# Expert one-hots of a PEER layer in 16-bit token pairs on VectorE, with a ScalarE copy of the left one, on one Trainium2 core

## The chip, the core and the metric

The kernel runs on one core of a Trainium2 chip. The metric is the device time of one execution, in microseconds (us). Of the core's engines four compute here: TensorE (PE in the profile; PEld is its weight load), VectorE (DVE), ScalarE (ACT) and GpSimd (POOL). The queue of SyncE (SP) streams weights, and some transfers are issued from the ACT and POOL queues.

## What is computed

A first block (feed-forward, token mixer, feed-forward) and then two layers of attention with a product-key expert layer ("PEER") run on 256 tokens of width 1024. The change touches the expert layer, plus the table of distances that the attention adds. Cut to what matters:

```python
PEER_HEADS, PEER_NKEYS, PEER_TOPK = 8, 128, 16        # 128 * 128 experts
scores = einsum("thpd,hpnd->thpn", q, sub_keys)       # two halves p of a key
top_v, top_i = lax.top_k(scores, PEER_TOPK)
cand_v = top_v[:, :, 0, :, None] + top_v[:, :, 1, None, :]
best_v, best_pos = lax.top_k(cand_v, PEER_TOPK)       # 16 experts per head
expert_idx = take_along_axis(cand_i, best_pos)        # = i0 * 128 + i1
gates = softmax(best_v)
a = gelu(einsum("td,thkd->thk", h, expert_u[expert_idx]))
y = einsum("thk,thkd->td", gates * a, expert_v[expert_idx])
```

## The kernel before

The kernel gathers no expert. It computes all 128 x 128 of them densely: weights arrive as units of 128x1024 f32, each is split into a high part (`w_hi`, by ScalarE, L390, called from `hi`) and the rest (`w_lo`, by VectorE, L728, called from `lo`), and TensorE multiplies high and low parts with the high and low parts of the activations (`product`, L1443, L1444 and L1447, for U; `v_unit`, L1837 and L1843, for V). There are two buffers of each, so `step(u)` on ScalarE and VectorE is the split of unit u+2: ScalarE's waits until TensorE has used unit u (`used`), VectorE's for ScalarE's (`w_hi_ready`), and TensorE's low pass for VectorE's (`w_taken`). The expert activations of a layer fill the arena, `experts[partition i0][n = i1][token]`.

What makes the dense sum the reference's is a matrix of gates: for each token a 128 x 128 matrix over (i0, i1) that holds the gate at the 128 chosen experts (8 heads x 16) and zero elsewhere. It is the product of two one-hot matrices over those 128 choices, made by TensorE for one token at a time: the left one (128 choices x 128 values of i0) is the stationary operand, the right one (128 choices x 64 values of i1, one half of the keys), weighed by the gate, is the moving operand. The gate is split in three bf16 parts, so there are three matmuls per token (L1811, 128x64). Tokens are taken in groups of 8, 32 groups to a half of the keys; a group is called a turn. Every turn goes with two weight units, and a layer has four stages:

- peer_a: U units 0 to 63, beside the top-k on VectorE.
- peer_b: U units 64 to 127, with 32 turns that make the gates of keys 0 to 63 and multiply them into `experts`. These are the u turns.
- peer_c: V units 0 to 63, with 32 turns for keys 64 to 127. These are the v turns.
- peer_d: V units 64 to 127, without turns.

In a turn of the kernel before, VectorE builds the right one-hot `hot_eq` (128x512) and the left one-hot `hot_l` (128x1024) by comparing f32 keys with f32 numbers (`build`, L1237); GpSimd multiplies `hot_eq` by the three gate parts (`weigh`, L1417); TensorE makes 24 matmuls (`token_gates`, L1811), and VectorE multiplies their result into `experts` (`multiply`, L1247). There is one buffer of `hot_l`, `hot_eq` and `hot_r`; the result has two (the banks `st` 2 and 3). The result lies token by token, 64 keys in a row each, while `experts` has the tokens in a row and the next key 256 elements on.

The orders are written by hand. VectorE in a u turn g (`u_turn`, L1264): right one-hot, `lo` of unit 2g+2, multiply of turn g-1, left one-hot, `lo` of unit 2g+3. In a v turn (`v_turn`, L1273) the low part of the activations, `lower` (L1253), stands before the right and before the left one-hot. TensorE (`turns`): unit 2g, gates of turn g-1, unit 2g+1, unit 2g+2, gates of turn g, unit 2g+3, and so on. ScalarE in a u turn: per unit a Gelu (L657) and a `hi` (L390); in a v turn: per unit a copy of the activations' high part, `upper` (L691), and a `hi`.

Of the kernel before, what the change touches and what calls it, by code (L numbers as in the profile page):

```python
# [92 lines left out]
def _layout1():  # L93
    at = 0
    for name, n in (("ident", 128), ("ones", 128), ("iota", 128), ("dist", TT * T), ("onecol", 31),
                    ("iota16", 16), ("eps", 1), ("qk_scale", 1), ("qk_eps", 1)):
        _K1[name] = (at, n)
        at += n
    return at
# [20 lines left out]
EXTRA = 3328  # L120


def build(nc, weights, ada_weights, params, const1, const2, smallw, out):
    with ExitStack() as ctx:
# [44 lines left out]
        def ar(at, *shape, base=None):  # L169
# [4 lines left out]
            elif len(shape) == 3:  # L174
# [11 lines left out]
        dist = kc("dist")  # L186
# [97 lines left out]
        selt = ar(512, 3, T, base=extra)  # L284

        gate_rest = ar(1280, 2, T, base=extra)
        gate_parts = ar(1792, 384, base=extra).bitcast(BF16).rearrange("p (k t) -> p k t", k=3)
        hot_l = ar(2176, 512, base=extra).bitcast(BF16).rearrange("p (t n) -> p t n", t=GROUP)
        hot_eq = ar(2688, 256, base=extra).bitcast(BF16).rearrange("p (t n) -> p t n", t=GROUP)
        hot_r = [ar(at, 256, base=extra).bitcast(BF16).rearrange("p (t n) -> p t n", t=GROUP)  # L290
                 for at in (2944, 1280, 1536)]
# [89 lines left out]
        def _(eng):  # L381
            link = linker(eng, "act_chain")
            nc_a = nc.scalar
            eng.dma_start(k1[:, :], const1).then_inc(sem("k1_in"), 16)
# [202 lines left out]
            for l in range(LAYERS):  # L587
# [83 lines left out]

                def gates_exp():
# [10 lines left out]
                u_half(HALF)  # L683
# [9 lines left out]
                def v_half(first):  # L693
# [3 lines left out]
                    with eng.Fori(0, HALF // 4 - 1) as i:  # L697
                        for k in range(4):
                            eng.wait_ge(used, plus(i, 4, nth(v_base + first + k)))
                            upper(first + k + 2, i)  # L700
                            step(v_base + first + k, i, 4)

                    for n in range(first + HALF - 4, first + HALF):
# [3 lines left out]
                        step(v_base + n)  # L707

                v_half(0)
# [10 lines left out]
        def _(eng):  # L720
# [335 lines left out]
            for l in range(LAYERS):  # L1056
# [9 lines left out]
                stage(eng, ST[f"proj{l}"])  # L1066
                for h in range(AH):
# [158 lines left out]
                def build(k, half, g, i=None):  # L1226
# [765 lines left out]
```

## Time and profile before

| | us |
|---|---|
| median of 3 runs | 3389.08 (3388.97 to 3389.96) |
| profiled execution, own time | 3391.32 |
| its span in the trace | 3389.6 |
| busy: PE, PEld | 3020.5 (89%), 2756.0 (81%) |
| busy: DVE, ACT, POOL | 2484.9 (73%), 1358.3 (40%), 750.7 (22%) |
| stages peer_b of the two layers (turns with U) | about 1543 to 1763 and 2726 to 2950 |
| stages peer_c (turns with V) | about 1771 to 2008 and 2958 to 3195 |
| mean granted TensorE clock | 0.935 of full speed |

The span is the time from the first to the last instruction in the trace; the execution's own time is 1.7 us longer. An engine's busy time is the union of its instructions. Idle time of an engine is given with what ended it. The stages above are found by where the one-hot instructions (L1237) begin and end.

### The profile page before, as it was taken

To read this page: it belongs to the slowest core of one execution; us is meant where nothing else is said; L and a number is where in the kernel's file an instruction comes from. 1 tells how busy PE (TensorE), PEld (TensorE's weight loads), DVE (VectorE), ACT (ScalarE), POOL (GpSimd) and SP (SyncE) were. 2 spreads that over 40 slices of the span, in tenths; PEclk is the share of its full clock that TensorE was granted. 3 is DMA by queue.
4 is the path that set the end of the run, shared out by engine and by line. 5 is a ranking of instruction groups with operands and counts; after the bars stand their busy time and mean duration, and the time that the engine had idled before them with its cause. 6 is when DMAs were issued, how large, how long until landed. Compare 5 with 4: busy or idle time off the path is not lost. (4 is left out here: it accounts for less than half of the span.)

```text
span 3389.6 us, 62057 instructions
## 1 busy us (share of the span) xinstructions
PE 3020.5 (89%) x22464; PEld 2756.0 (81%) x22464; DVE 2484.9 (73%) x3349; ACT 1358.3 (40%) x1958; POOL 750.7 (22%) x588
## 2 busy tenths in 40 slices
PE   3998988889989778999998889998799999988898
PEld 2998976779979578989987668796799899866687
DVE  6777734357778566998999986644449889899865
ACT  2434532234344334544333335543345443333354
POOL 1011002101101000025765530000000256655300
PEclk7999986889989689999999999997899999999999
DMA  7784520048858345544444445552245444444454
GB/s 270 270 278 139 185 100 1 1 147 276 278 199 316 103 153 176 174 159 144 153 137 148 137 143 192 166 171 78 100 148 174 156 149 149 136 146 139 143 192 143
DMA packets 149585, 547.98 MB, mean 162 GB/s; under 512 B 16608, under 2 KB 16736, under 8 KB 149088
## 3 DMA queue, kind: packets, MB, share of 16 engines
q1 hardware_dynamic: 124704, 454.29, 39.8%
q0 software_dynamic: 24336, 89.14, 7.8%
q10 hardware_dynamic: 432, 2.97, 0.2%
q8 instruction: 79, 1.29, 0.2%
q14 instruction: 34, 0.28, 0.0%
HBM read 545.29 MB, written 1.05 MB: 161 GB/s over the span
## 5 line engine op out<-in xcount | busy, mean ns | idle before, releaser
L728 DVE TENSOR_TENSOR w_lo<-ring,w_hi 128x1024 fp32r<-128x1024 f32 x864 | 1140.4, 1321 | 542.8 <-ACT w_hi L390 539.9
L390 ACT ACTIVATE w_hi<-ring 128x1024 fp32r<-128x1024 f32 x864 | 910.8, 1054 | 1105.7 <-PE st L1447 915.6
L1443 PE MATMUL st<-h_hi,w_hi 128*128 128x256 f32 x4064 | 1038.7, 292 | 43.1 <-DVE h_lo L757 27.0
L1444 PE MATMUL st<-h_lo,w_hi 128*128 128x256 f32 x4064 | 1016.6, 287 | 0.0
L1443 PEld LDWEIGHTS st<-h_hi,w_hi 128*128 128x128 f32 x4064 | 793.7, 195 | 62.8 <-issue 38.6
L1444 PEld LDWEIGHTS st<-h_lo,w_hi 128*128 128x128 f32 x4064 | 796.2, 196 | 1.0
L1417 POOL TENSOR_TENSOR extra<-extra 128x512 bf16<-128x512 bf16 x384 | 565.7, 1499 | 429.5 <-DVE extra L1237 429.5
L1447 PE MATMUL st<-h_hi,w_lo 128*128 128x256 f32 x4064 | 581.9, 287 | 23.1 <-DVE w_lo L728 22.8
L1447 PEld LDWEIGHTS st<-h_hi,w_lo 128*128 128x128 f32 x4064 | 532.7, 195 | 29.5 <-DVE w_lo L728 29.3
L1237 DVE TENSOR_TENSOR extra<-extra,k 128x512 bf16<-128x512 f32 (+1 forms) x256 | 334.1, 1305 | 5.3 <-PE st L1811 2.8
L1837 PE MATMUL acc<-w_hi,act_hi 128*128 128x512 f32 x1024 | 325.4, 399 | 4.9 <-DVE act_lo L1253 4.9
L1837 PE MATMUL acc<-w_hi,act_lo 128*128 128x512 f32 x1024 | 319.5, 393 | 0.0
L691 ACT ACTIVATE act_hi<-arena 128x256 fp32r (+1 forms) x256 | 106.6, 418 | 487.1 <-PE acc L1843 470.5
L1843 PE MATMUL acc<-w_lo,act_hi 128*128 128x512 f32 x1024 | 275.5, 391 | 0.0
L1332 POOL DMA_DIRECT2D arena<-ada_weights x156 | 82.4, 528 | 815.1 <-DVE arena L782 443.9
L1837 PEld LDWEIGHTS acc<-w_hi,act_lo 128*128 128x128 f32 x1024 | 194.5, 190 | 41.5
L1843 PEld LDWEIGHTS acc<-w_lo,act_hi 128*128 128x128 f32 x1024 | 193.9, 189 | 41.1
L1837 PEld LDWEIGHTS acc<-w_hi,act_hi 128*128 128x128 f32 x1024 | 189.7, 191 | 42.7 <-issue 5.1
L1253 DVE TENSOR_TENSOR act_lo<-arena,act_hi 128x256 fp32r<-128x256 f32 x256 | 127.9, 501 | 117.1 <-ACT act_hi L691 114.7
L1811 PEld LDWEIGHTS st<-extra 128*128 128x128 bf16 x3072 | 97.6, 98 | 118.4 <-issue 94.2
L1811 PE MATMUL st<-extra 128*128 128x64 bf16 x3072 | 112.4, 194 | 79.4 <-DVE extra L1237 68.8
L1247 DVE TENSOR_TENSOR arena<-arena,st 128x512 f32 (+1 forms) x128 | 170.9, 1335 | 0.8 <-PE st L1811 0.8
(254 smaller groups left out, 3060.4 us busy)
## 6 DMA issues: line engine op xcount, KB each, us to landing
ring<-weights SPq DMA_DIRECT2D x864, 512.0 KB, 3.3
arena<-ada_weights POOLq DMA_DIRECT2D x168, 512.0 KB, 5.1
arena<-const ACTq DMA_DIRECT2D x1, 2112.0 KB, 8.7
x_t<-params SPq DMA_DIRECT2D x1, 1024.0 KB, 8.3
out<-arena POOLq DMA_DIRECT2D x1, 1024.0 KB, 4.2
k<-const ACTq DMA_DIRECT2D x1, 473.0 KB, 4.6
arena<-smallw ACTq DMA_DIRECT2D x1, 320.0 KB, 10.4
par<-params SPq DMA_DIRECT2D x1, 198.5 KB, 4.4
```

Source lines behind the costliest of these rows:

```text
L390: nc_a.activation(w_hi[:, u % 2, :], ring[:, u % RING, :], ACT.Copy).then_inc(hi_ready, 1)
L728: v.tensor_tensor(w_lo[:, u % 2, :], ring[:, u % RING, :], w_hi[:, u % 2, :], ALU.subtract)\
L1237: v.tensor_tensor(dst, selt[:, k, at].unsqueeze(2).to_broadcast([P, GROUP, width]), numbers.unsqueeze(1).to_broadcast([P, GROUP, width]), ...
L1247: v.tensor_tensor(here, here, st[:, 2 + g % 2, :].rearrange("p (t n) -> p t n", t=GROUP), ALU.mult).then_inc(sem("g_mult"), 1)
L1253: v.tensor_tensor(act_lo[:, n % 2, :], src, act_hi[:, n % 2, :], ALU.subtract) .then_inc(sem("gated_lo"), 1)
L1417: g.tensor_tensor(hot_r[k], hot_eq, gate_parts[:, k, at].unsqueeze(2) .to_broadcast([P, GROUP, HALF]), ALU.mult).then_inc(sem("hot_r"), 1)
L1443: mm(dst(t), w, hi_t(t), start=start, stop=False, skip_group_check=True)
L1444: mm(dst(t), w, lo_t(t), start=False, stop=False, skip_group_check=True)
L1447: ins = mm(dst(t), w_lo[:, u % 2, t * P:(t + 1) * P], hi_t(t), start=False, stop=last and (t == DT - 1 or not shared), skip_group_check=True)
L1811: ins = mm(st[:, 2 + g % 2, k * HALF:(k + 1) * HALF], hot_l[:, k, :], hot_r[part_][:, k, :], start=part_ == 0, stop=part_ == 2)
L1837: mm(acc[:, 2 * t + half, :], act_part[:, b, t * P:(t + 1) * P], w_hi[:, u % 2, 512 * half:512 * half + 512], start=False, stop=False, ski ...
L1843: ins = mm(acc[:, 2 * t + half, :], act_hi[:, b, t * P:(t + 1) * P], w_lo[:, u % 2, 512 * half:512 * half + 512], start=False, stop=last, ...
```

## The change

Both one-hots become bf16 throughout. Keys are copied out of PSUM as bf16 (`keys_t`), the numbers 0 to 127 are kept twice side by side in bf16 (`pair_iota`), and two tokens lie innermost in each one-hot, `[4 pairs of tokens][keys][2 tokens]`. The weighing moves from GpSimd to VectorE (`weigh`, three products of 128x512), and there are two buffers of the weighed right one-hots and of the left one. The left one-hot is built in pairs too (`hot_pair`, one buffer), and ScalarE copies it into rows that are contiguous per token (`by_token`), from which TensorE loads its weights. TensorE reads the right one-hot in steps of two elements and writes the result with the 8 tokens innermost, in steps of 8 f32, so that `multiply` runs over tokens in rows of 8. The table of distances moves out of the constants that stay loaded: it is loaded at the beginning of each attention layer into the arena, from the POOL queue, and VectorE waits for it (`dist_in`). The diff, cut:

```diff
-EXTRA = 3328
+EXTRA = 3840
+DIST_AT = 26112
...
-        dist = kc("dist")
+        dist = ar(DIST_AT, TT * T)
...
+        hot_l = [ar(512 * b, 512, base=extra).bitcast(BF16).rearrange("p (t n) -> p t n", t=GROUP) for b in range(2)]
+        hot_r = [[hots(1024 + 768 * b + 256 * k, 256) for k in range(3)] for b in range(2)]
+        hot_pair = hots(3328, 512)
...
+        keys_t = ar(2944, 256, base=extra).bitcast(BF16).rearrange("p (k t) -> p k t", k=2)
+        pair_iota = ar(3200, 128, base=extra).bitcast(BF16).rearrange("p (n r) -> p n r", r=2)
...
-            eng.dma_start(k1[:, :], const1).then_inc(sem("k1_in"), 16)
+            eng.dma_start(k1[:, :], const1[:, 0:N_K1]).then_inc(sem("k1_in"), 16)
...
+                def by_token(half, g, i=None):
+
+                    n = 2 * TURNS * l + TURNS * half + g
+                    eng.wait_ge(sem("hot_pair"), plus(i, 2, n + 1))
+                    if n >= 2:
+                        eng.wait_ge(sem("g_psum"), plus(i, 2, n - 1))
+                    nc_a.activation(hot_l[g % 2].rearrange("p (q r) n -> p q n r", r=2), hot_pair, ACT.Copy)\
+                        .then_inc(sem("hot_l"), 1)
...
                             gelu_of(first + k, i)
                             step(base + first + k + 1, i, 4)
+                            if turns and k % 2 == 0:
+                                by_token(0, k // 2, i)
...
-                nc_a.activation(selt, st[:, 2:4, :].rearrange("p a b -> p (a b)")[:, 0:3 * T]
-                                .rearrange("p (k t) -> p k t", k=3), ACT.Copy).then_inc(sem("selt"), 1)
+                nc_a.activation(keys_t, st[:, 2, :].rearrange("p (k t) -> p k t", k=2), ACT.Copy)
+                nc_a.activation(gate_t, st[:, 3, 0:T], ACT.Copy).then_inc(sem("selt"), 1)
...
                             upper(first + k + 2, i)
                             step(v_base + first + k, i, 4)
+                            if turns and k % 2 == 1:
+                                by_token(1, k // 2, i)
...
+                eng.wait_ge(sem("dist_in"), 16 * (l + 1))
...
+                def spread(row, g, i, n):
+
+                    return row[:, tokens(g, i)].rearrange("p (q r) -> p q r", r=2).unsqueeze(2)\
+                        .to_broadcast([P, GROUP // 2, n, 2])
+
+                def right(half, g, i=None):
...
+                    v.tensor_tensor(hot_r[b][0], spread(keys_t[:, 1, :], g, i, HALF),
+                                    numbers.unsqueeze(1).to_broadcast([P, GROUP // 2, HALF, 2]), ALU.is_equal)\
+                        .then_inc(sem("hot_eq"), 1)
+
+                def weigh(half, g, i=None):
...
+                    for k in (1, 2, 0):
+                        ins = v.tensor_tensor(hot_r[b][k], hot_r[b][0], spread(gate_parts[:, k, :], g, i, HALF), ALU.mult)
+                    ins.then_inc(sem("hot_r"), 1)
+
+                def left(half, g, i=None):
+
+                    n = 2 * TURNS * l + TURNS * half + g
+                    if n >= 1:
+                        eng.wait_ge(sem("hot_l"), plus(i, 2, n))
+                    v.tensor_tensor(hot_pair, spread(keys_t[:, 0, :], g, i, NKEYS),
+                                    pair_iota.unsqueeze(1).to_broadcast([P, GROUP // 2, NKEYS, 2]), ALU.is_equal)\
+                        .then_inc(sem("hot_pair"), 1)
...
                 def multiply(half, g, i=None):
...
-                    here = experts[:, HALF * half:HALF * half + HALF, at].rearrange("p n t -> p t n")
-                    v.tensor_tensor(here, here, st[:, 2 + g % 2, :].rearrange("p (t n) -> p t n", t=GROUP),
+                    here = experts[:, HALF * half:HALF * half + HALF, tokens(g, i)]
+                    v.tensor_tensor(here, here, st[:, 2 + g % 2, :].rearrange("p (n t) -> p n t", t=GROUP),
                                     ALU.mult).then_inc(sem("g_mult"), 1)
...
                 def u_turn(half, g, i=None):
                     u = base + HALF + 2 * g
-                    build(1, half, g, i)
+                    right(half, g, i)
                     step(u, i, 4)
+                    weigh(half, g, i)
                     if g > 0:
                         multiply(half, g - 1, i)
-                    build(0, half, g, i)
+                    left(half, g, i)
                     step(u + 1, i, 4)
...
                 eng.wait_ge(sem("selt"), l + 1)
-                link(v.tensor_copy(gate_parts[:, 0, :], selt[:, 2, :]))
+                v.tensor_copy(pair_iota, kc("iota").unsqueeze(2).to_broadcast([P, NKEYS, 2]))
+                link(v.tensor_copy(gate_parts[:, 0, :], gate_t))
...
+                eng.dma_start(dist, const1[:, N_K1:N_K1 + TT * T]).then_inc(sem("dist_in"), 16)
...
-                    for k in range(3):
-                        g.tensor_tensor(hot_r[k], hot_eq, gate_parts[:, k, at].unsqueeze(2)
-                                        .to_broadcast([P, GROUP, HALF]), ALU.mult).then_inc(sem("hot_r"), 1)
...
-                            ins = mm(st[:, 2 + g % 2, k * HALF:(k + 1) * HALF], hot_l[:, k, :],
-                                     hot_r[part_][:, k, :], start=part_ == 0, stop=part_ == 2)
+                            ins = mm(st[:, 2 + g % 2, :].rearrange("p (n t) -> p n t", t=GROUP)[:, :, k],
+                                     hot_l[g % 2][:, k, :], hot_r[g % 2][part_][:, k // 2, :, k % 2],
+                                     start=part_ == 0, stop=part_ == 2)
```

The v turn changes in the same way (`right` and `left` for the two builds, `weigh` behind the first `step`).

How the orders move is seen in two places. The first is VectorE in the last turn of peer_b. Before (L1237 is a one-hot, L728 a `lo`, L1247 a multiply):

```order
L1237 TENSOR_TENSOR extra<-extra,k 128x512
L728 TENSOR_TENSOR w_lo<-ring,w_hi 128x1024
L1247 TENSOR_TENSOR arena<-arena,st 128x8x64
L1237 TENSOR_TENSOR extra<-extra,k 128x1024
L728 TENSOR_TENSOR w_lo<-ring,w_hi 128x1024
L1247 TENSOR_TENSOR arena<-arena,st 128x8x64
```

The same turn now (L1268 is the right one-hot, L750 a `lo`, L1278 the weighing, L1295 a multiply, L1286 the left one-hot):

```order
L1268 TENSOR_TENSOR extra<-extra 128x512
L750 TENSOR_TENSOR w_lo<-ring,w_hi 128x1024
L1278 TENSOR_TENSOR extra<-extra 128x512 x3
L1295 TENSOR_TENSOR arena<-arena,st 128x64x8
L1286 TENSOR_TENSOR extra<-extra 128x1024
L750 TENSOR_TENSOR w_lo<-ring,w_hi 128x1024
L1295 TENSOR_TENSOR arena<-arena,st 128x64x8
```

Three instructions come in ahead of the multiply and the left one-hot, and the multiply's inner dimension is now 8 tokens.

The second place is ScalarE in the loop over v turns, one turn. Before (L691 is `upper`, L390 is `hi`; ISA and REGISTER_ALU are instructions of the queue that prepare addresses and counts):

```order
L691 ACTIVATE act_hi<-arena 128x256
L390 ACTIVATE w_hi<-ring 128x1024
```

The same turn now (L709 is `upper`, L395 is `hi`, L670 the copy by token):

```order
L709 ACTIVATE act_hi<-arena 128x256
L395 ACTIVATE w_hi<-ring 128x1024
L667 ISA
L669 REGISTER_ALU
L670 ACTIVATE extra<-extra 128x4x128x2
L717 REGISTER_ALU
L709 ISA
L709 ACTIVATE act_hi<-arena 128x256
```

The copy stands behind the second `hi` of each turn and ahead of the next `upper`; in a u turn it stands likewise behind a `hi` and ahead of a Gelu. GpSimd's queue has no instruction of the turns left, and one transfer more per layer.

## Rows read from the trace of the kernel before

**Rows 1.** Busy time by stage: peer_b and peer_c of the first layer.

```profile
1543.00:1762.00 219.00, 213.23 (x2291) 207.04 (x2291) 213.82 (x159) 85.19 (x128) 152.42 (x96) 1.00 0.47 151
1771.00:2005.00 234.00, 201.20 (x1498) 160.19 (x1496) 228.69 (x221) 86.44 (x126) 130.33 (x96) 1.00 0.43 141
```

**Rows 2.** Chain that ended last, second layer: start us, us, what.

```profile
2802.27 2.06 DVE w_lo L728
...
2809.14 2.06 DVE w_lo L728
...
2976.90 2.07 DVE extra L1237
...
2984.27 2.07 DVE extra L1237
...
3203.32 1.81 PE acc L1837 x8
...
3206.04 1.81 PE acc L1837 x8
```

**Rows 3.** Groups by line and shape, whole run: count, busy us, mean ns, idle before.

```profile
L1237 DVE TENSOR_TENSOR extra<-extra,k 128x1024 bf16<-128x1024 f32 x128 | 246.4, 1925 | 0.0
L1247 DVE TENSOR_TENSOR arena<-arena,st 128x512 f32 x120 | 160.7, 1340 | 0.0
L1009 DVE TENSOR_TENSOR extra<-extra,acc 128x512 f32<-128x512 f32 x24 | 16.4, 682 | 4.0 <-PE acc L1634 4.0
L390 ACT ACTIVATE w_hi<-ring 128x1024 fp32r<-128x1024 f32 x864 | 910.8, 1054 | 1105.7 <-PE st L1447 915.6 <-PE acc L1447 155.8 <-DMA ring<-weights 13.6
```

**Rows 4.** Order of time, one u turn: start us, us, engine, instruction, [idle before].

```profile
1700.91 0.19 PEld L1443 LDWEIGHTS st<-h_hi,w_hi 128*128 128x128 f32 x1
...
1701.27 0.69 DVE L1237 TENSOR_TENSOR extra<-extra,k 128x512 bf16<-128x512 f32 x1
...
1701.88 1.22 DVE L728 TENSOR_TENSOR w_lo<-ring,w_hi 128x1024 fp32r<-128x1024 f32 x1
...
1702.16 4.82 POOL L1417 TENSOR_TENSOR extra<-extra 128x512 bf16<-128x512 bf16 x3 [1.98 <-DVE extra L1237]
...
1703.77 0.19 PEld L1443 LDWEIGHTS st<-h_hi,w_hi 128*128 128x128 f32 x1
...
1704.09 1.06 ACT L390 ACTIVATE w_hi<-ring 128x1024 fp32r<-128x1024 f32 x1 [2.58 <-PE st L1447]
...
1707.02 0.76 PEld L1811 LDWEIGHTS st<-extra 128*128 128x128 bf16 x24 [0.30 <-POOL extra L1417]
...
1707.71 0.19 PEld L1443 LDWEIGHTS st<-h_hi,w_hi 128*128 128x128 f32 x1
```

**Rows 5.** Order of time, one v turn.

```profile
1803.11 0.62 PE L1837 MATMUL acc<-w_hi,act_hi 128*128 128x512 f32 x2
...
1804.66 2.06 DVE L1237 TENSOR_TENSOR extra<-extra,k 128x1024 bf16<-128x1024 f32 x1
...
1806.13 0.42 ACT L691 ACTIVATE act_hi<-arena 128x256 fp32r x1 [1.35 <-PE acc L1843]
1806.45 1.04 ACT L390 ACTIVATE w_hi<-ring 128x1024 fp32r<-128x1024 f32 x1
...
1806.94 0.87 PE L1811 MATMUL st<-extra 128*128 128x64 bf16 x24 [0.95 <-DVE extra L1237]
...
1807.65 0.70 PE L1837 MATMUL acc<-w_hi,act_hi 128*128 128x512 f32 x2
...
1810.50 0.61 PE L1837 MATMUL acc<-w_hi,act_hi 128*128 128x512 f32 x2
```

**Rows 6.** The page's DMA issues: line, engine, count, KB each, us to landing.

```profile
ring<-weights SPq DMA_DIRECT2D x864, 512.0 KB, 3.3
...
k<-const ACTq DMA_DIRECT2D x1, 473.0 KB, 4.6
```

More of the change, by code:

```diff
@@ L94, in _layout1 @@
     at = 0
[L95 removed]
+    for name, n in (("ident", 128), ("ones", 128), ("iota", 128), ("onecol", 31),
                     ("iota16", 16), ("eps", 1), ("qk_scale", 1), ("qk_eps", 1)):
@@ L657, in gelu_of, with u_half @@
                     nc_a.activation(dst, st[:, n % 2, 0:T], ACT.Gelu_apprx_tanh).then_inc(sem("gelu"), 1)
-                def u_half(first, between=None):
+                def by_token(half, g, i=None):
[5 more added lines that the diff above has]
+                        .then_inc(sem("hot_l"), 1)
+                def u_half(first, between=None, turns=False):
                     step(base + first)
@@ L670, in u_half @@
                             step(base + n + 1)
+                        if turns and n % 2 == 0:
+                            by_token(0, (n - first) // 2)
                 def gates_exp():
@@ L691, in upper, with v_half @@
                     nc_a.activation(act_hi[:, n % 2, :], src, ACT.Copy).then_inc(sem("gated_hi"), 1)
-                def v_half(first):
+                def v_half(first, turns=False):
                     v_base = base + NKEYS
@@ L707, in v_half @@
                         step(v_base + n)
-                v_half(0)
+                        if turns and n % 2 == 1:
+                            by_token(1, (n - first) // 2)
+                v_half(0, turns=True)
                 stage(eng, ST[f"peer_c{l}"])
@@ L1276, in v_turn @@
                         lower(2 * g + 2, i)
-                    build(1, half, g, i)
+                    right(half, g, i)
                     step(u, i, 4)
+                    weigh(half, g, i)
                     if g > 0:
@@ L1282, in v_turn @@
                         lower(2 * g + 3, i)
-                    build(0, half, g, i)
+                    left(half, g, i)
                     step(u + 1, i, 4)
                 eng.wait_ge(sem("selt"), l + 1)
-                link(v.tensor_copy(gate_parts[:, 0, :], selt[:, 2, :]))
-                link(v.tensor_tensor(gate_rest[:, 0, :], selt[:, 2, :], gate_parts[:, 0, :], ALU.subtract))
+                v.tensor_copy(pair_iota, kc("iota").unsqueeze(2).to_broadcast([P, NKEYS, 2]))
+                link(v.tensor_copy(gate_parts[:, 0, :], gate_t))
+                link(v.tensor_tensor(gate_rest[:, 0, :], gate_t, gate_parts[:, 0, :], ALU.subtract))
                 link(v.tensor_copy(gate_parts[:, 1, :], gate_rest[:, 0, :]))
@@ L1904, in _constants @@
                  qk_eps=np.where(is_q, 128e-6, 1e-6))
-    k1 = np.concatenate([parts[n] for n in _K1], 1).astype(np.float32)
+    k1 = np.concatenate([parts[n] for n in _K1] + [parts["dist"]], 1).astype(np.float32)
     j, i = f[:, None], f[None, :]
```

40 lines of the change are left out of this document (16 added, 24 removed).

## The prediction

> **What bounds the kernel now.** The change works in the turns, so I read by stage, not the page's shares. The table by stage [rows 1] (after the span: PE, PEld, DVE, ACT, POOL busy, then the clock) shows DVE busy 213.8 of 219 us and PE 213.2 in peer_b, and DVE 228.7 of 234 against PE 201.2 in peer_c: with U both engines are full, with V only DVE is. ACT has 85 to 86 us in each. The clock is full, so nothing is to be had there. The chain that ended last [rows 2] repeats once per turn: a `lo` of 2.06 us every 6.87 us in peer_b, the left one-hot of 2.07 us every 7.37 us in peer_c. In peer_d the chain is PE alone, 2.72 us per V unit; that stage is out of reach.
>
> One u turn [rows 4]: unit at 1700.91, next at 1703.77 (2.86 us each), gates at 1707.02, next unit at 1707.71. The turn is 6.80 us, the gates are 0.69 of it, and PE stands idle for 0.30, for POOL's weighing, which takes 4.82 us. While POOL runs, DVE's instructions are long: `lo` is 1.22 us in one place and 2.06 in another [rows 2, 4]. The mean of the two layers' turns is 6.83. One v turn [rows 5]: gates from 1806.94 to 1807.65 (0.71), the unit behind them 2.85, the other 2.72, and 0.95 to 1.1 us of waiting for the left one-hot: 7.37. TensorE's own need is thus 6.50 (6.80 less 0.30) and 6.28 us per turn. There are 32 turns x 2 layers = 64 of each sort, so 0.01 us in both sorts is 1.3 us of the run. At best PE alone would bind: 64 x (0.33 + 1.09) = 91 us.
>
> **The change part by part.**
> POOL's weighing goes (4.82 us per turn), with the wait for it and the long DVE instructions beside it.
>
> DVE gains three weighings and loses length elsewhere. 512 elements take 0.69 us, 1024 take 1.22 [rows 4]: 1.04 ns an element and 0.16 fixed. For the new 16-bit instructions the trace has no row. Upper bound: the same rate, 0.69 and 1.22. Lower bound: two elements at a time, (0.16 + 256 x 1.04 ns) = 0.42 and 0.69. I take the lower, since every operand now has neighbouring 16-bit pairs. Multiply takes 1.34 us where it hops 1 KB from key to key, and a 128x512 product with one PSUM operand but contiguous rows takes 0.68 [rows 3]; with rows of 8 I take 0.68. Successive instructions overlap by some 0.07. A v turn on DVE is then 0.35 + 2 x 1.14 + 3 x 0.35 + 0.61 + 0.61, and two `lower`s of 0.35: 5.6 us, a u turn 4.9, both under PE's need. The edit to DVE stops being a bound, unless the pairs don't engage (rival 4).
>
> What is late next is ScalarE. `by_token` is one copy of 1024 elements per turn. TensorE waits for it before the gates of that same turn, and it can't begin before the `hi` of unit 2g+3, which waits for unit 2g+1 to be used. Behind it on ACT stand a Gelu or `upper` and the next `hi`. In a v turn: unit 2g+1 ends at 1803.11 + 2.72 = 1805.83, `upper` starts 0.30 later, `hi` 0.32 after that, and lasts 1.04 [rows 5]; the copy starts at +1.57 (0.30 + 0.32 + 0.95, with a little overlap), and its end must reach PE, for which I take 0.1. PE meanwhile has only unit 2g+2, 2.72 us. In a u turn `hi` starts 0.32 after the unit's end (1704.09 less 1703.77) [rows 4], the copy at +1.27, against 2.86. So a copy of up to 1.05 us (v) or 1.5 us (u) is hidden, and what it takes beyond that is paid in each of 64 turns.
>
> Its duration is the term that decides. Lower bound: ACT's copy of 1024 contiguous elements, 1.05 us (L390) [rows 3]. But it writes neighbours in turn to two rows 256 B apart. The one hopping access in the trace is multiply's: 1.34 against 0.68 us for 512, 1.3 ns more per element, with both a read and the write hopping [rows 3]. Half of that for one side is 1.05 + 0.65 = 1.70, all of it 2.36. I take 1.9: the per-element part of L390 (1.05 less the 0.2 that is fixed by the 0.42 of a 256-element copy [rows 5]) doubled, as in multiply. Turns are then: u 0.69 + 2.86 + (1.27 + 1.9 + 0.1) = 6.82, v 0.71 + 2.85 + (1.57 + 1.9 + 0.1) = 7.13. The Gelu behind the copy ends at +3.6, while PE needs it after the gates, at +3.96.
>
> TensorE's gates: the moving operand steps by 4 B, the output by 32 B. No row has such matmuls. Bounds: 0.69 us per turn as now, or double. I take 0.69, and rivals 2 and 3 hold the rest. The Trainium skill, "Advanced Engine Details and Errata", section Memory Cachelines, has a rule against each of the two accesses: in SBUF an access that goes to another 16-byte line each time is penalised, and for PSUM it says "Any non-contiguous AP significantly slows down matmuls". By the first, the copy is slow, as I take it and as multiply's row agrees; by the second the gates are too, and the sum would be that of rival 3.
>
> Small terms. Two pair-number copies and one more ACT instruction per layer, under 2 us in all. The first constants shrink by 256 KB of 473 KB, which land in 4.6 us [rows 6]; up to 1 us earlier, half of it taken. The distances (256 KB; 512 KB land in 3.3 us [rows 6]) are asked for a whole projection stage before their wait, so that wait costs nothing; on POOL's queue they stand ahead of one ring of ada loads for one issue, also nothing. Without that cover they would cost 3 us per layer.
>
> Sum: 64 x (6.82 - 6.83) + 64 x (7.13 - 7.37) = -16 us, small terms +1: 3391.3 - 15 = 3376 for the profiled execution, which is 2.2 us above the median: **3374 us**.
>
> **The rivals.**
> Rival 1, *nothing hops dearly*: the copy takes 1.05 us. Then v turns are held by DVE's chain over two turns (from the end of unit 2g: `hi` 1.66, `lo`, weighing, multiply, `lower`, left one-hot to 5.6, copy to 6.8; two turns cannot take less than 6.28 + 6.8), 6.54 us, and u turns by PE, 6.50. 64 x (-0.33 - 0.83) = -74, and with the small terms and the way to the median 3316. For it: ACT has 85 of 219 us of work, and 16-bit writes are half as wide. Against: the multiply row.
> Rival 2, *only the gates' output hops dearly*: gates 1.4 us, u 7.20, v 6.98; 64 x (0.37 - 0.39) = -1: 3389.
> Rival 3, *both do*, the one on the slower side: gates 1.4 us stand in the same loop as the 1.9 us copy. u 7.53, v 7.83; 64 x (0.70 + 0.46) = +74: 3464. It decides for slower once copy and gates together exceed today's by enough: with gates at 0.7 the copy must be over 2.0 us; with the copy at 1.9 us each 0.1 us of gates costs 13 us, so 0.12 us more is enough. The page's PSUM rule named above is this rival's ground; no row here speaks for or against it.
> Rival 4, *the 16-bit pairs don't run two at a time*: DVE's instructions are 0.69 and 1.22 us, its v turn 7.2 us, and its chain over two turns 1.3 to 1.6 us longer; with the 1.9 us copy u is 7.3 and v 7.65: 64 x (0.47 + 0.28) = +48: 3438. The Trainium skill, "VectorE: DVE Perf Modes", section The perf-mode tier table, states two results a cycle for bf16 `tensor_tensor` in SBUF, which would rule this rival out; the trace has no such instruction.
>
> **How the numbers follow.** Chances: forecast 0.32, rival 1 0.26, rival 2 0.10, rival 3 0.23, rival 4 0.09. The forecast's own range, by a copy of 1.7 to 2.36 us, is 3349 to 3433, with three parts in four below no change. I call 0.2% (7 us) no change, about what a measurement of this kernel can tell. Faster: 0.26 + 0.24 + 0.03 = 0.53. Within: 0.02 + 0.05 = 0.07. Slower: 0.23 + 0.09 + 0.06 + 0.02 = 0.40. The range reaches from a little under rival 1, 3305, to rival 3 with a little on it, 3470.
>
> **What would show it.** The copy's row (128x1024 on ACT, 64 x 2 of it) at 1.9 us; the three weighings at about 0.42 us, multiply at 0.7, every `lo` at 1.22; the 24 gate matmuls still within 0.7 us from first to next unit; PE idle before the gates some 0.3 to 0.9 us per turn and ended by ACT, not DVE; peer_d unchanged at 2.72 us per unit. A copy at 1.05 us, or gates at 1.4 us, makes the prediction wrong, and says which rival holds.

## The result and the profile after

The changed kernel takes **4041.42 us** (median of 4 runs, 4039.41 to 4041.63), against 3389.52 (3388.97 to 3391.70, 4 runs) for the kernel before beside it: a ratio of 1.1921, 95% interval 1.19 to 1.1941. The forecast was 3374, in a range up to 3470. The profiled execution took 4039.41 us, its span is 4037.7.

The page of the changed kernel, its busy times, the granted clock in slices, and the two groups (L670 is the copy by token, L1853 the gates' matmuls):

```profile
PE 3294.1 (82%) x22464; PEld 3007.2 (74%) x22464; DVE 2278.3 (56%) x3735; ACT 1936.6 (48%) x2088; POOL 186.2 (5%) x206
...
PEclk8999878998969998999777799978999998777799
...
L1853 PE MATMUL st<-extra 128*128 128x64 bf16 x3072 | 289.7, 307 | 457.5 <-ACT extra L670 457.5
...
L670 ACT ACTIVATE extra<-extra 128x1024 bf16<-128x1024 bf16 x128 | 609.4, 4761 | 21.7 <-DVE extra L1286 21.6
```

GpSimd's 750 us have gone to 186 and VectorE has 207 us less, as meant. But ScalarE's copy lasts 4.76 us, and TensorE stood idle for it 457.5 us in 128 places, 3.6 us each. PE's busy time rose by 274 us with the same number of matmuls. Of that, 63 us is there at the full clock too (3083.4 in experiment 2), by the gates' longer matmuls; the other 211 go with the lower clock.

VectorE's groups by line and shape show what went as meant (L1278 weighing, L1286 left one-hot, L1295 multiply, L1268 right one-hot):

```profile
L1278 DVE TENSOR_TENSOR extra<-extra 128x512 bf16<-128x512 bf16 x384 | 139.4, 418 | 0.0
...
L1286 DVE TENSOR_TENSOR extra<-extra 128x1024 bf16<-128x1024 bf16 x128 | 87.6, 684 | 0.0
L1295 DVE TENSOR_TENSOR arena<-arena,st 128x512 f32 x120 | 81.6, 680 | 0.0
...
L1268 DVE TENSOR_TENSOR extra<-extra 128x512 bf16<-128x512 bf16 x128 | 53.6, 419 | 0.1
```

Against [rows 3] the left one-hot fell from 1.925 to 0.68 us and the multiply from 1.34 to 0.68.

The same two stages as in [rows 1], first layer, in the table by stage:

```profile
1545.00:1880.00 335.00, 240.47 (x2249) 234.06 (x2247) 158.78 (x254) 225.08 (x159) 0.00 (x0) 0.96 0.29 99
1892.00:2260.00 368.00, 260.25 (x1297) 214.47 (x1295) 156.28 (x272) 197.56 (x137) 0.00 (x0) 0.75 0.23 77
```

VectorE is busy under half the time now. ACT is busy 225 of 335 us, without being full: the copy, not ScalarE's load, is what TensorE waits for. In peer_c the granted clock is 0.75, where the kernel before had 1.00: for half of that stage's time TensorE ran at 1.2 GHz instead of 2.4.

**One u turn after**, in order of time. What answers to [rows 4] is this:

```profile
1756.98 1.51 PE L1853 MATMUL st<-extra 128*128 128x64 bf16 x24 [2.96 <-ACT extra L670]
...
1758.30 0.36 PE L1485 MATMUL st<-h_hi,w_hi 128*128 128x256 f32 x1
...
1761.25 0.28 PE L1485 MATMUL st<-h_hi,w_hi 128*128 128x256 f32 x1
...
1761.45 1.06 ACT L395 ACTIVATE w_hi<-ring 128x1024 fp32r<-128x1024 f32 x1 [3.10 <-PE st L1489]
...
1762.41 4.77 ACT L670 ACTIVATE extra<-extra 128x1024 bf16<-128x1024 bf16 x1
```

The gates take 1.32 us from first to next unit (0.69 before), and the unit behind them ends at 1761.25. The next gates start at 1767.24, so the turn is 10.26 us: 1.32 + 2.95 + 1.16 until the copy starts + 4.77 + 0.06. That is the loop that the prediction wrote down.

**One v turn after**, TensorE and then ScalarE and VectorE, answering to [rows 5]:

```profile
1902.74 2.74 PE L1853 MATMUL st<-extra 128*128 128x64 bf16 x24 [4.24 <-ACT extra L670]
1905.24 1.20 PE L1880 MATMUL acc<-w_hi,act_hi 128*128 128x512 f32 x2
...
1909.65 0.61 PE L1880 MATMUL acc<-w_hi,act_hi 128*128 128x512 f32 x2
...
1909.95 0.42 ACT L709 ACTIVATE act_hi<-arena 128x256 fp32r x1 [6.19 <-PE acc L1886]
...
1910.51 0.43 DVE L1301 TENSOR_TENSOR act_lo<-arena,act_hi 128x256 fp32r<-128x256 f32 x1 [3.88 <-ACT act_hi L709]
...
1910.86 0.68 DVE L1286 TENSOR_TENSOR extra<-extra 128x1024 bf16<-128x1024 bf16 x1
...
1911.65 4.75 ACT L670 ACTIVATE extra<-extra 128x1024 bf16<-128x1024 bf16 x1 [0.33 <-DVE extra L1286]
...
1916.53 2.74 PE L1853 MATMUL st<-extra 128*128 128x64 bf16 x24 [3.99 <-ACT extra L670]
```

This turn is 13.79 us: gates 2.50, unit 4.41, 2.00 until the copy starts, 4.75 of copy, 0.13. Two things here are in no step of the prediction. TensorE stands still for 4 us, and then the gates and the unit behind them run at the lower clock: 2.50 and 4.41 us, against 1.31 and 2.84 where the clock stays full (experiment 2); the second unit, 2.7 us, is at full speed again. And the copy starts 2.00 us after the unit's end, not 1.57: the left one-hot stands behind `lower` (L1301) on VectorE, which waits for `upper` (L709), which waits for the unit.

**The sum closes.** From the first gates of the first layer's u turns to the last (1552.97 to 1883.34, 31 turns) a turn is 10.66 us on average, since seven of them meet the lower clock and last over 11.7; in the second layer (3057.91 to 3403.88) it is 11.16, with 17 such turns. The v turns are 13.63 (1902.74 to 2325.27) and 13.55. The same stretches of the kernel before have 6.79 and 6.86, and 7.35 in both layers. Between first and last gates of the four stages that is 31 x (3.87 + 4.30 + 6.28 + 6.20) = 640 of the 648 us by which the span grew; the other 8 lie around the stages' ends.

### The profile page after: what moved, and what is told of

The parts are those of the page before. It is cut to its first block and busy times, and to the rows that moved or that the text cites. A ratio compares the mean times of both kernels' runs of the same rounds, so it can differ in the third digit from the quotient of the medians.

```text
span 4037.7 us, 62103 instructions
## 1 busy us (share of the span) xinstructions
PE 3294.1 (82%) x22464; PEld 3007.2 (74%) x22464; DVE 2278.3 (56%) x3735; ACT 1936.6 (48%) x2088; POOL 186.2 (5%) x206
## 3 DMA queue, kind: packets, MB, share of 16 engines
HBM read 545.55 MB, written 1.05 MB: 135 GB/s over the span
## 5 line engine op out<-in xcount | busy, mean ns | idle before, releaser
L750 DVE TENSOR_TENSOR w_lo<-ring,w_hi 128x1024 fp32r<-128x1024 f32 x864 | 1087.2, 1260 | 930.5 <-ACT w_hi L395 924.2
L395 ACT ACTIVATE w_hi<-ring 128x1024 fp32r<-128x1024 f32 x864 | 910.1, 1053 | 1082.9 <-PE st L1489 890.3
L1853 PE MATMUL st<-extra 128*128 128x64 bf16 x3072 | 289.7, 307 | 457.5 <-ACT extra L670 457.5
L1853 PEld LDWEIGHTS st<-extra 128*128 128x128 bf16 x3072 | 260.5, 157 | 496.9 <-issue 362.3
L670 ACT ACTIVATE extra<-extra 128x1024 bf16<-128x1024 bf16 x128 | 609.4, 4761 | 21.7 <-DVE extra L1286 21.6
L1301 DVE TENSOR_TENSOR act_lo<-arena,act_hi 128x256 fp32r<-128x256 f32 x256 | 108.5, 425 | 566.4 <-ACT act_hi L709 566.4
L709 ACT ACTIVATE act_hi<-arena 128x256 fp32r (+1 forms) x256 | 123.8, 485 | 558.0 <-PE acc L1886 544.0
L1880 PE MATMUL acc<-w_hi,act_hi 128*128 128x512 f32 x1024 | 379.5, 457 | 3.8 <-DVE act_lo L1301 3.8
L1880 PE MATMUL acc<-w_hi,act_lo 128*128 128x512 f32 x1024 | 354.5, 430 | 0.0
L1880 PEld LDWEIGHTS acc<-w_hi,act_hi 128*128 128x128 f32 x1024 | 222.8, 225 | 47.9 <-issue 4.3
L1485 PE MATMUL acc<-h_hi,w_hi 128*128 128x256 f32 x416 | 115.9, 310 | 54.5 <-DVE h_lo L769 26.1
L1278 DVE TENSOR_TENSOR extra<-extra 128x512 bf16<-128x512 bf16 x384 | 139.4, 418 | 0.0
L1485 PEld LDWEIGHTS acc<-h_hi,w_hi 128*128 128x128 f32 x416 | 89.5, 215 | 57.8 <-DVE h_lo L769 26.7
```

Source lines behind the costliest of these rows:

```text
L395: nc_a.activation(w_hi[:, u % 2, :], ring[:, u % RING, :], ACT.Copy).then_inc(hi_ready, 1)
L670: nc_a.activation(hot_l[g % 2].rearrange("p (q r) n -> p q n r", r=2), hot_pair, ACT.Copy)\
L709: nc_a.activation(act_hi[:, n % 2, :], src, ACT.Copy).then_inc(sem("gated_hi"), 1)
L750: v.tensor_tensor(w_lo[:, u % 2, :], ring[:, u % RING, :], w_hi[:, u % 2, :], ALU.subtract)\
L1278: ins = v.tensor_tensor(hot_r[b][k], hot_r[b][0], spread(gate_parts[:, k, :], g, i, HALF), ALU.mult)
L1301: v.tensor_tensor(act_lo[:, n % 2, :], src, act_hi[:, n % 2, :], ALU.subtract) .then_inc(sem("gated_lo"), 1)
```

## Experiments

Each kernel is compared with the kernel before on the same chip: 3390.70 us (11 runs) for experiments 1 to 4, 3390.32 (15 runs) for 5 to 8. My theory after the result: the copy is slow because its write goes to two rows in turn, whatever the width of the elements, and the gates are slow because their output steps. The rivals were that a 16-bit write, or a 16-bit read with a step, is slow in any order, that the reading of the moving operand in steps slows the gates, and that contention, not the access, lengthens the copy.

### 1. Single instructions, by themselves

The kernel before, with rows of instructions added at the beginning of peer_d, on buffers that are free by then. Each of ACT's is made twice:

```diff
+hop = dst.rearrange("p (q r n) -> p q n r", q=4, r=2)
...
+    link(nc_a.activation(dst, src, ACT.Copy))
+    link(nc_a.activation(hop, src.rearrange("p (q n r) -> p q n r", q=4, r=2), ACT.Copy))
...
+for k in range(24):
+    mm(o[:, 0:128].rearrange("p (n t) -> p n t", t=2)[:, :, 0], w0, m0, start=True, stop=True)
```

> The kernel before with rows added between the last turn of the first layer and its peer_d stage, to price single accesses (it computes what before computes, and its total time says nothing). ScalarE copies of 1024 elements. Theory A (the hopping write is what is slow): dense to dense 1.05 us; the change's form (writes alternating between rows 256 B apart) 4.8 us, also in f32; reading with a step of 4 B and writing dense 1.05 us; runs of 2 elements between hops about half of the hop's cost, runs of 8 near 1.1 us. Theory B (a 16-bit write, or a 16-bit read with a step, is slow in any order): dense to dense in bf16 or the stepped read is near 4.8 us too, and f32 is not. VectorE's copies of the same forms: by either theory dense under 1.05, the hopping write 2.4 us or more. TensorE, 24 matmuls of 128x64 bf16 each: Theory A (stepped PSUM output): dense 0.7 us, output step 8 and output step 2 1.3 us, pairs between hops nearer 0.7, moving step 2 0.7, weights with step 2 0.7 to 1.3. Theory B (stepped moving operand): moving step 2 is 1.3 us and output step 8 is 0.7.

The instructions by line (count: shortest/median/longest in ns, first and last start, shape). ACT: L718 dense, L719 the change's copy, L720 the same elements written in the output's order (reads step 4 B), L721 L719's pattern in f32 (its rows lie 512 B apart, L719's 256 B), L722 writes step 4 B, L723 jumps between two rows with two neighbours at each jump (these rows lie 1 KB apart), L725 hopping reads with a dense write. Then DVE: L1322 dense, L1323 the change's pattern, L1325 that in f32:

```profile
L718 ACT ACTIVATE extra<-extra x2: 1056/1056/1056, 2008.4 to 2022.2; 128x1024 bf16<-128x1024 bf16 x2
L719 ACT ACTIVATE extra<-extra x2: 4710/4736/4761, 2009.5 to 2023.3; 128x1024 bf16<-128x1024 bf16 x2
L720 ACT ACTIVATE extra<-extra x2: 1056/1056/1057, 2014.3 to 2028.0; 128x1024 bf16<-128x1024 bf16 x2
L721 ACT ACTIVATE extra<-extra x2: 1972/1990/2007, 2015.4 to 2029.1; 128x1024 f32<-128x1024 f32 x2
L722 ACT ACTIVATE extra<-extra x2: 1341/1342/1342, 2017.4 to 2031.1; 128x1024 bf16<-128x1024 bf16 x2
L723 ACT ACTIVATE extra<-extra x2: 1087/1088/1089, 2018.8 to 2032.5; 128x1024 bf16<-128x1024 bf16 x2
L725 ACT ACTIVATE extra<-extra x2: 1169/1170/1170, 2021.0 to 2034.7; 128x1024 bf16<-128x1024 bf16 x2
L1322 DVE COPY extra<-extra x2: 427/427/427, 2037.0 to 2042.1; 128x1024 bf16<-128x1024 bf16 x2
L1323 DVE COPY extra<-extra x2: 2734/2736/2737, 2037.5 to 2042.6; 128x1024 bf16<-128x1024 bf16 x2
L1325 DVE COPY extra<-extra x2: 1071/1076/1080, 2041.0 to 2046.1; 128x1024 f32<-128x1024 f32 x2
```

The second of the two L719 copies (2023.27) ran while TensorE, VectorE and GpSimd stood idle and no DMA moved, and it still took 4.71 us, so contention is out. The same elements read with steps and written in order cost nothing (L720), and hopping reads cost 0.11 us (L725): it is the *write* in turn to two rows that takes 1.05 us to 4.74, or (4.74 - 0.2) / 1024 = 4.4 ns an element. My theory had f32 at 4.8 us too; it took 1.99, 1.75 ns an element, and two neighbouring 16-bit elements at each jump took 1.09. VectorE shows the same pair, 2.74 and 1.08 us.

That the single 16-bit element at each jump is what costs is the nearest reading, and it isn't shown: the three patterns also differ in how far apart their rows lie (256 B, 512 B, 1 KB), and no run has single 16-bit elements in turn to rows at another distance. That they are single isn't enough by itself: written 4 B apart (L722) they take 1.34. The Trainium skill, "Advanced Engine Details and Errata", section Memory Cachelines, wants "at least two hits on a cacheline"; L723 with two neighbours agrees. That rule alone would set L719 and L721 alike, and they differ by 2.4 times; the section adds that the tolerance depends on the element type, without saying how.

TensorE, 24 matmuls of 128x64 in each row (L1887 dense; L1889 output in steps of 8; L1891 moving operand in steps of 2; L1893 weights in steps of 2; L1895 output hopping, but in pairs; L1897 output in steps of 2; L1899 dense):

```profile
2008.42 1.46 PE L1887 MATMUL st<-extra 128*128 128x64 bf16 x24 [1.38 <-DVEq L319]
2009.69 2.75 PE L1889 MATMUL st<-extra 128*128 128x64 bf16 x24
2012.20 1.09 PE L1891 MATMUL st<-extra 128*128 128x64 bf16 x24
2013.12 0.86 PE L1893 MATMUL st<-extra 128*128 128x64 bf16 x24
2013.82 0.86 PE L1895 MATMUL st<-extra 128*128 128x64 bf16 x24
2014.52 1.50 PE L1897 MATMUL st<-extra 128*128 128x64 bf16 x24
2015.83 0.89 PE L1899 MATMUL st<-extra 128*128 128x64 bf16 x24
```

From start to start: weights in steps and output in pairs 0.70 us, as dense gates do in the kernel before (0.69 [rows 4]); output in steps of 2 takes 1.31. The first two rows ran at the lower clock (a dense 24 in 1.27, a stepped 24 in 2.51), and the clock rose in the third, so these give only a ratio: again two. A step in the output doubles the gates, at a step of 2 as of 8. The moving operand in steps of 2 has no row at a settled clock here; in experiment 4 the gates have it and take 0.73 us, so it isn't what slows them.

### 2. The copy walked in its output's order

```diff
-nc_a.activation(hot_l[g % 2].rearrange("p (q r) n -> p q n r", r=2), hot_pair, ACT.Copy)
+nc_a.activation(hot_l[g % 2].rearrange("p (q r) n -> p q r n", r=2),
+                hot_pair.rearrange("p q n r -> p q r n"), ACT.Copy)
```

> The change with the ScalarE copy walked in the order of its output, so that it writes dense rows and reads with a step of 4 B. Theory A (hopping write): the copy takes 1.05 us, is hidden behind the second unit of the turn, TensorE's clock stays full in the v turns, gates take 1.3 us: u turn 7.04, v turn 6.9, and about 3373 us in all. Theory B (16-bit copy slow in any order): copy 4.8 us, 4041 us as the change.

3399.81 us (3397.53 to 3402.29, 8 runs), ratio 1.0025, interval 1.0015 to 1.0036. This one line, with the same elements read and written, is worth 642 us. The group of its copy, its v turns in the table by stage, and one v turn in order of time:

```profile
L670 ACT ACTIVATE extra<-extra 128x1024 bf16<-128x1024 bf16 x128 | 134.4, 1050 | 21.6 <-DVE extra L1287 21.5
```

```profile
1790.00:2000.00 210.00, 201.20 (x1375) 163.57 (x1374) 163.76 (x286) 108.57 (x145) 0.00 (x0) 1.00 0.43 142
```

```profile
1903.59 1.51 PE L1854 MATMUL st<-extra 128*128 128x64 bf16 x24 [0.30 <-ACT extra L670]
1904.90 0.70 PE L1881 MATMUL acc<-w_hi,act_hi 128*128 128x512 f32 x2
...
1907.74 0.61 PE L1881 MATMUL acc<-w_hi,act_hi 128*128 128x512 f32 x2
...
1909.74 1.06 ACT L670 ACTIVATE extra<-extra 128x1024 bf16<-128x1024 bf16 x1 [0.33 <-DVE extra L1287]
```

The copy is 1.05 us, and with it the clock is back at 1.00: gates 1.31, the unit behind them 2.84. So the lower clock in the changed kernel's v turns is a consequence of TensorE's waits for the copy. By the averages of both layers, 64 x (3.13 + 3.71) = 438 of the 642 us are the shorter copy (in u turns 3.13 of the 3.71 us, since with it TensorE's own work becomes the longer path), and 64 x (0.63 + 2.56) = 204 are the clock. The u turn is 7.15 us (TensorE's own need with gates of 1.32; it is busy throughout), the v turn 1.31 + 2.84 + 2.00 + 1.06 + 0.12 = 7.33. I had expected 3373 since I still let the copy start at +1.57: 64 x 0.43 = 28 us are the wait for `lower` told above. The u turn, 0.1 longer than my 7.04, adds 6, and the stretches around the stages' ends came out 8 shorter than in the kernel before.

### 3. The gates' output dense, the slow copy kept

```diff
-ins = mm(st[:, 2 + g % 2, :].rearrange("p (n t) -> p n t", t=GROUP)[:, :, k],
+ins = mm(st[:, 2 + g % 2, k * HALF:(k + 1) * HALF],
...
-here = experts[:, HALF * half:HALF * half + HALF, tokens(g, i)]
-v.tensor_tensor(here, here, st[:, 2 + g % 2, :].rearrange("p (n t) -> p n t", t=GROUP),
+here = experts[:, HALF * half:HALF * half + HALF, tokens(g, i)].rearrange("p n t -> p t n")
+v.tensor_tensor(here, here, st[:, 2 + g % 2, :].rearrange("p (t n) -> p t n", t=GROUP),
```

> The change with only the gates' output dense again (and the multiply hopping), the slow copy kept. Theory A: gates 0.7 us in u turns and 1.3 us in v turns at the lower clock, instead of 1.3 and 2.5; 64 x (0.6 + 1.2) = 115 us less than the change, 3925 us. If the gates are hidden behind the copy, no change: 4041 us.

3995.98 us (one run), only 45 less than the changed kernel's, where I had expected 115. The stages: a u and a v stretch of the first layer (the first in the same window as above), and the u turns of the second, of which the changed kernel's row comes last:

```profile
1545.00:1880.00 335.00, 243.42 (x2182) 237.39 (x2181) 170.09 (x246) 217.10 (x152) 0.00 (x0) 0.85 0.29 96
1950.00:2200.00 250.00, 170.96 (x958) 136.88 (x959) 126.52 (x200) 144.10 (x101) 0.00 (x0) 0.77 0.26 84
3100.00:3400.00 300.00, 215.27 (x1843) 207.44 (x1842) 143.19 (x204) 186.43 (x131) 0.00 (x0) 0.82 0.27 89
```

```profile
3100.00:3430.00 330.00, 236.74 (x2050) 227.09 (x2048) 148.26 (x239) 210.57 (x150) 0.00 (x0) 0.92 0.27 92
```

The v turns went from 13.63 to 12.47 us (1916.47 to 2303.18, 31 turns), by nearly half of the 2.50 us that their gates took at the lower clock, and in the second layer from 13.55 to 12.48. But the u turns went *up*, from 10.66 to 11.13 and from 11.16 to 11.41, though their gates have half the work: the clock there fell from 0.96 to 0.85 and from 0.92 to 0.82. 31 x (0.47 + 0.25 - 1.16 - 1.07) = -47 us, and -45 was measured. With the waits of 3 to 4 us left in each turn, less work between them went with a lower clock, and that took back a part. By an estimate from the gates at full clock (1.32 against 0.73 us) they would be worth 64 x 2 x 0.6 = 77 us without that.

### 4. Both: the copy in order and the output dense

The edits of experiments 2 and 3 together.

> As e1_rows, and the gates' matmuls write dense rows of PSUM as before, with the multiply hopping as before (1.34 us). Theory A: gates 0.7 us per turn, TensorE's own need is all that binds in u turns (6.5 us), v turns 6.3 to 6.6 us with VectorE at 6.3; 3315 to 3335 us. Theory B on the gates (the stepped moving operand makes them long): gates still 1.3 us, about 3375 us.

3343.23 us (3339.36 to 3344.84, 4 runs), ratio 0.9855, interval 0.9839 to 0.9872: faster than the kernel before. Gates are 0.73 us, the u turn 6.56 and the v turn 6.87. My 3315 to 3335 was missed by 8 us, since I had v turns at 6.6 at most. In one of them, VectorE's multiply and `lower`, then the copy (the unit before it ended at 1902.27):

```profile
1902.02 1.35 DVE L1296 TENSOR_TENSOR arena<-arena,st 128x512 f32 x1
1903.29 0.40 DVE L1302 TENSOR_TENSOR act_lo<-arena,act_hi 128x256 fp32r<-128x256 f32 x1
...
1904.41 1.06 ACT L670 ACTIVATE extra<-extra 128x1024 bf16<-128x1024 bf16 x1 [0.47 <-DVE extra L1287]
```

The multiply hops again, 1.35 us against 0.68, and `lower` now stands behind it: the copy starts 2.14 us after the unit's end and not 2.00, which costs 64 x 0.14 = 9 us in the v turns and nothing in the u turns, where TensorE has no wait. Of the hopping that the change took from VectorE and gave to TensorE, TensorE's side was by far the dearer: the exchange brings 3400 to 3343, 57 us.

### 5. No copy: TensorE reads the pairs

```diff
-hot_l = [ar(512 * b, 512, base=extra).bitcast(BF16).rearrange("p (t n) -> p t n", t=GROUP) for b in range(2)]
+hot_l = [hots(512 * b, 512) for b in range(2)]
...
-                                by_token(0, k // 2, i)
...
-v.tensor_tensor(hot_pair, spread(keys_t[:, 0, :], g, i, NKEYS),
+v.tensor_tensor(hot_l[g % 2], spread(keys_t[:, 0, :], g, i, NKEYS),
...
-         hot_l[g % 2][:, k, :], hot_r[g % 2][part_][:, k // 2, :, k % 2],
+         hot_l[g % 2][:, k // 2, :, k % 2], hot_r[g % 2][part_][:, k // 2, :, k % 2],
```

The output is dense as in experiment 3. VectorE's two buffers of the left one-hot need no wait of their own.

> The change without any ScalarE copy: two buffers of the paired left one-hot, from which TensorE loads its weights with a step of 2 elements, and the gates' output dense in PSUM as before. Theory A (the copy's scattered 16-bit writes and the stepped PSUM output were the whole loss, stepped weights are free, as the added rows showed with 0.7 us for 24): no wait for ScalarE before the gates, u turn 6.5, v turn 6.3 to 6.4 where VectorE's own 6.3 us of work is as long as TensorE's 6.28: 3295 to 3310 us. Theory C (stepped weights are dear in the loop, which is why there was a copy): gates 1.3 us, about 3380 us.

**3301.39 us** (3300.91 to 3301.77, 5 runs), ratio 0.9737, interval 0.9724 to 0.9751: the fastest version. The group of its gates, and its turn stages:

```profile
L1843 PE MATMUL st<-extra 128*128 128x64 bf16 x3072 | 115.1, 193 | 6.4 <-DVE extra L1276 6.4
```

```profile
1550.00:1740.00 190.00, 190.00 (x2073) 188.75 (x2070) 160.95 (x232) 76.69 (x116) 0.00 (x0) 1.00 0.48 160
1760.00:1960.00 200.00, 199.20 (x1503) 162.36 (x1501) 195.66 (x315) 86.78 (x126) 0.00 (x0) 1.00 0.49 163
```

TensorE is busy 190.0 of 190 and 199.2 of 200 us: it waits for nothing. The turns average 6.54 and 6.26 us, and 64 x (0.29 + 1.11) = 90 us is the whole gain (89 measured). These are the 6.50 and 6.28 that the prediction gave as TensorE's own need, and loading weights in steps of 2 costs nothing. The copy, ScalarE's share of the change, was not needed at all.

### 6. VectorE writes the left one-hot per token

```diff
-v.tensor_tensor(hot_pair, spread(keys_t[:, 0, :], g, i, NKEYS),
-                pair_iota.unsqueeze(1).to_broadcast([P, GROUP // 2, NKEYS, 2]), ALU.is_equal)
+v.tensor_tensor(hot_l[g % 2],
+                keys_t[:, 0, tokens(g, i)].unsqueeze(2).to_broadcast([P, GROUP, NKEYS]),
+                pair_iota[:, :, 0].unsqueeze(1).to_broadcast([P, GROUP, NKEYS]), ALU.is_equal)
```

No copy, dense output, and the one-hot loses its pairs.

> As e4, but VectorE writes the left one-hot dense per token, one element at a time (1.22 instead of 0.68 us), as before the change, in 16 bits. Theory A: u turn 6.5, v turn 6.8 by VectorE's sum (0.54 us more than in e4): about 3335 us. If VectorE isn't what binds the v turns of e4, it equals e4.

3325.10 us (3322.40 to 3325.52, 4 runs), ratio 0.9805, interval 0.979 to 0.982. The one-hot takes 1.24 us instead of 0.68, which puts a wait of 0.2 us before the gates of v turns (6.68 us). The left one-hot's pairs are worth 24 us when nothing undoes them.

### 7. The distances alone

The kernel before, with the distances loaded per layer into the arena and waited for, as in the change (`DIST_AT`, `dist_in`, the first constants cut to `N_K1`).

> The kernel before with the change's reload of the distances alone (two 256 KB transfers on the POOL queue, and the first constants 256 KB smaller). By the prediction's small term: within 1 us of before, rather earlier by 0.5 us. Rival: the wait for the distances shows, 3 us per layer later.

3389.52 us (3388.78 to 3392.06, 11 runs), ratio 0.9998, interval 0.9989 to 1.0007. The reload takes 2.9 us under the projection and costs nothing.

### 8. The kernel before with stepped output

```diff
-ins = mm(st[:, 2 + g % 2, k * HALF:(k + 1) * HALF], hot_l[:, k, :],
+ins = mm(st[:, 2 + g % 2, :].rearrange("p (n t) -> p n t", t=GROUP)[:, :, k], hot_l[:, k, :],
```

and the multiply over rows of 8, as in the change.

> The kernel before with the change's PSUM layout alone: gates written in steps of 8 f32, multiply in rows of 8. Theory A: gates 1.3 instead of 0.7 us per turn, multiply 0.68 instead of 1.34. In u turns TensorE needs 7.1 us, 0.3 more than the turn had: +18 us; in v turns VectorE, which binds there, gains up to 0.66 us but its waits for TensorE grow, 6.9 to 7.4 us: 0 to -30 us. In all 3380 to 3410 us. If the gates took no longer there, it would be 3389 - 42 = 3347 us.

3523.19 us (3520.40 to 3525.33, 4 runs), ratio 1.0393, interval 1.0377 to 1.0409: far above what I expected, by 113 us at the least. A u turn in order of time:

```profile
1608.91 1.51 PE L1811 MATMUL st<-extra 128*128 128x64 bf16 x24 [1.11 <-POOL extra L1417]
...
1611.46 5.80 POOL L1417 TENSOR_TENSOR extra<-extra 128x512 bf16<-128x512 bf16 x3 [2.61 <-DVE extra L1237]
```

The turn is 8.41 us. With a single buffer the right one-hot can't be built before the gates have read it, GpSimd's weighing follows the one-hot, and the gates follow the weighing: a loop through three engines in which a longer gate stands whole. The gates take 1.32 us here (0.63 more), and the weighing grew by 0.98, from 4.82 to 5.80; together that is the 1.61 by which the turn grew. The v turn went from 7.35 to 7.90. Between first and last gates of the stages, 62 x (1.62 + 0.54) = 134 us of the 133 measured. Why the weighing grew wasn't tried; beside the v turns' instructions it takes 4.02 us in both kernels.

The kernel before has the same loop, and it closes there without slack. VectorE's `lo` and the next right one-hot, behind the gates of [rows 4]:

```profile
1706.00 2.06 DVE L728 TENSOR_TENSOR w_lo<-ring,w_hi 128x1024 fp32r<-128x1024 f32 x1
1708.06 0.69 DVE L1237 TENSOR_TENSOR extra<-extra,k 128x512 bf16<-128x512 f32 x1
```

From this one-hot to the weighing 0.89 us, 4.82 of weighing, 0.04 to the gates, and 1.04 from their start to the next one-hot: 6.79, the whole turn. VectorE's own order leaves no idle time there either, so the two held the u turn together, and a longer gate was not hidden behind anything. The second buffer and the weighing's move end the loop; what each is worth alone wasn't tried.

## Why the prediction was wrong

**The reading of the bound was right.** ScalarE's copy is late next, and it stands in a loop with the gates and one unit. The two turn formulas (gates + unit + start of the copy + copy + 0.1) describe the traces; what was put into them was wrong. Where the 667 us between 3374 and 4041 come from:

| term | forecast | measured | us in all |
|---|---|---|---|
| the copy, both turns | 1.9 | 4.76 | 128 x 2.86 = 366 |
| the lower clock, v turns | none | 13.59 a turn, 2.56 of it | 64 x 2.56 = 164 |
| the lower clock, u turns | none | 10.91 a turn, not 10.28 | 64 x 0.63 = 40 |
| gates' stepped output at full clock | 0.69, 0.71 | 1.32, 1.31 | 64 x 1.23 = 79 |
| start of the copy, v and u | 1.57, 1.27 | 2.00, 1.16 | 64 x (0.43 - 0.11) = 20 |
| unit behind the gates, u | 2.86 | 2.95 | 64 x 0.09 = 6 |

Together 675 us, 8 more than there are: the table counts 64 turns of each sort, and from first to last gates there are 62. (13.59 and 10.91 are averages of both layers; 2.56 is what 13.59 leaves for the clock once 11.03 for the other terms is taken off.)

**The step that failed is the copy's duration.** The prediction put it at 1.9 us and bounded it by 1.05 below and 2.36 above, from multiply's hop [rows 3]; it took 4.76. That row is VectorE's, in f32, with 1 KB from one element to the next; the probe shows that f32 in this pattern on ScalarE is 1.99 us. The copy writes 16-bit elements in turn to rows 256 B apart, and nothing in the trace did that. I carried over a price per element from a row of another width and another distance and called its upper end a bound. It was none, and the range up to 3470 rested on it. Which of the two differences makes the price stays open.

**The copy's start in v turns** was a path I had wrong as well: the formula lets the copy follow `hi` at +1.57, and it follows VectorE's left one-hot, behind `upper` and `lower`, at +2.00.

**The gates' output** was a bound I had at both ends (0.69 or double), and the upper holds; rival 3 had this, and its price of 1.4 was near the 1.32. With the copy as forecast and a full clock the terms of the table would have given 3374 + 79 + 20 + 6 = 3479, already above the range. The Trainium skill's PSUM rule named in the prediction ("Any non-contiguous AP significantly slows down matmuls") agrees with the probe for single elements, twice the time at steps of 2 and 8; its "any" goes too far, since pairs with jumps between them cost nothing (0.70 us), as the same section's "Every two consecutive elements should be contiguous for best throughput" has it. Rival 2 (gates dear, copy not) is experiment 2: 3389 foretold, 3400 measured, with the u turn right (7.20 against 7.15) and the v turn short by its later start.

**The clock** is where the structure itself was incomplete. "The clock is full, so nothing is to be had there" holds for the kernel before, but the prediction never asked what a TensorE that idles 4 us in each turn is granted. It cost 204 us, more than the gates.

**What held.** VectorE's terms: 0.42 and 0.68 us for 16-bit pairs, the multiply at 0.68, `lo` beside nothing at 1.22 to 1.26; rival 4 is ruled out, and the Trainium skill's two results a cycle ("VectorE: DVE Perf Modes", The perf-mode tier table) agrees with these rows: 512 elements less a fixed 0.16 us are 0.26 us, half the 1.04 ns an element of before. TensorE's need of 6.50 and 6.28 (experiment 5). Rival 1's direction, since without the copy and the stepped output the gain is 89 us; its own case, a copy of 1.05 us and dense gates, is experiment 4, 3343 where it had 3316, short mainly by the later start of the copy. The distances at nothing (experiment 7). One reading of the rows did not hold as it was put: "while POOL runs, DVE's instructions are long". The `lo` of 1.22 us at 1701.88 [rows 4] runs for 0.94 us of it beside the weighing, so which of VectorE's instructions GpSimd lengthened isn't told by these rows.

## What to carry to other kernels

Before a step is put a second time into another layout, ask whether the reader can take the stride: here ScalarE's reads and TensorE's weight loads in steps of 4 B cost nothing, while 16-bit elements written in turn to two rows 256 B apart cost 4.5 times and a PSUM output in steps of single elements costs twice. If a copy must transpose, walk it in the order of its output. And a price taken from a row holds only for that row's width and distances: where they differ, the upper end stays open, the more so if the instruction stands in TensorE's loop, where waiting may cost clock on top.

## What was not expected of the hardware

- 16-bit elements written in turn to two rows 256 B apart are slower than 32-bit words written in turn to two rows 512 B apart: 4.74 against 1.99 us on ScalarE, 2.74 against 1.08 on VectorE, for 1024 elements a partition. With two neighbours at each jump, and rows 1 KB apart, ScalarE takes 1.09. Width and distance were not varied one at a time.
- The clock can take back what TensorE saves: less gate work in experiment 3 brought the granted clock of the u stages from 0.96 to 0.85 and from 0.92 to 0.82 and lengthened the turn by 0.47 and 0.25 us. It is one run of that kernel, the same way in both layers.
- GpSimd's weighing lengthened from 4.82 to 5.80 us in the u turns of experiment 8, which changed nothing in its own instructions, and stayed at 4.02 in the v turns. The cause is open.
